# The V product of a sparse-expert layer on TensorE: half of its float32 products split in three float32r products, and the loop around them rebuilt

## The chip, the core and the metric

The kernel runs on one core of one Trainium2 chip. The metric is the device time of one execution in microseconds (us), the median of several runs; lower is better. PE is TensorE, PEld its weight loads, DVE VectorE, ACT ScalarE, POOL GpSimd, and SP the engine that issues most DMAs.

## What is computed

One layer of an encoder runs on 1024 prompt positions and 64 sample positions: a modulated RMS norm, a mixing part (a gated recurrence and a state-space scan), and then a retrieval of experts with product keys. The retrieval is the part that matters here. Each position has 8 heads; each picks 16 of 16384 experts. An expert is one row `u` and one row `v` of 1024 numbers.

```python
gate = jax.nn.softmax(top_s, axis=-1)
act = jax.nn.gelu(jnp.einsum("nd,nhkd->nhk", xb, u_tab[eidx]).astype(jnp.float32))
coef = (gate * act).astype(xb.dtype)
return jnp.einsum("nhk,nhkd->nd", coef, v_tab[eidx])
```

The layer's output is the residual plus a gate times this sum, and a final RMS norm follows. All is float32.

## The kernel before

The time is spent in two parts. Up to about 1226 us the kernel makes everything ahead of the retrieval: mixing, keys, the choice of experts, a table of `u` rows turned round into DRAM, and for the positions that are handled densely a coefficient for each expert and position, stored in `coef_dram`. From 1226 us on one loop of 64 steps makes the retrieval, in two ways side by side.

**Dense way, 576 positions, on PE.** A step `t` takes two blocks of 128 experts, `e` = 0 and 1. Positions stand in two groups of columns, 320 and 256 wide (`DCHUNKS`). `scores(t, j)`, with j = 0 to 3 for the two blocks times the two groups, multiplies the block's `u` rows by the positions' vectors. It makes a float32 product out of three products of type float32r, one instruction each: high part by high part, low by high, high by low (8 x 3 products, line 975). ACT applies gelu from PSUM into the buffer `w` (line 1319), and DVE multiplies `w` by the coefficients (`weigh`). Then `values(g, wp, m)` multiplies the `v` rows of four blocks (two steps, a pair `g`) by `w`: for each of 8 pieces `d` of 128 output channels and each of the two column groups four products of type float32, which run as two instructions each (line 986). The sums lie in four PSUM banks in turn, and DVE adds each of the 16 to `y_sum` in SBUF (`add_up`). In PE's order each `scores(t, j)` is followed by two calls of `values`, one for each column group, of the pair before. I call such a piece, one `scores` and two `values`, a quarter of a step.

**Sparse way, 512 positions, on DVE.** In step `t` eight picks of 128 positions are done. POOL gathers for each the `u` row and the `v` row of every position from DRAM with an indirect DMA of 128 rows of 4 KB (line 599), into a ring of 4 slots for each table. DVE takes the dot product of the `u` row with the position's vector (`dot`, line 1927), ACT applies gelu, and DVE adds the weighted `v` row to `y_rows` (`add_row`, line 1941), one step later. POOL issues the gather for row p + 4 when row p has been used.

**What orders the work.** Every engine runs its program in the order in which it is written, and waits on semaphores. DVE's step interleaves, for each quarter, `weigh`, two `dot`, two `add_up`, two `add_row`; at the end of quarters 0 and 2 it makes the low part of the next `u` rows (`u_rest`, writes `u_lo`), for which ACT makes the high part (`u_first`). SP loads the raw `u` rows, the `v` rows and the coefficients of each step as buffers come free.

**The loop's start and end.** SP loads `u` of step 1 and `v` of steps 0 and 1 after the last coefficients have been stored. At the end PE makes the last 16 `values`; ACT scales `y_sum` by the layer's gate; PE turns the sums back into rows of positions; DVE adds them to the residual, ACT squares, and DVE scales the nine tiles of 128 positions for output.

Of the kernel before, what the change touches and what calls it, by code (L numbers as in the profile page):

```python
# [18 lines left out]
F32 = mybir.dt.float32  # L19
# [6 lines left out]
P = 128  # L26
DM = 1024
# [28 lines left out]
NLINK = 20  # L56
NCAND = 4 * 16 + 12 * 4
# [39 lines left out]
PQ, CB, ITR = 9216, 31232, 47616  # L97
YB, WR, CBD, VR = 31232, 35840, 40448, 42752
# [3 lines left out]
def trunk(nc, A, O):  # L102
    with ExitStack() as ctx:
# [8 lines left out]
        arena = sb("arena", [P, ARENA + NPACK])  # L112
# [20 lines left out]
        u_hi, u_lo = rounded("u_hi", UH, 2048), rounded("u_lo", UR, 2048)  # L133
        yl_hi, yl_lo = rounded("yl_hi", YLH, 4352), rounded("yl_lo", YL, 4352)
# [18 lines left out]
        rms4 = sb("rms4", [P, 30])  # L153
# [161 lines left out]
        def _(sp):  # L315
# [74 lines left out]
            load(ar(X1, 8192).rearrange("p (k d) -> p k d", k=8), A["xp"], "x_again_in")  # L390
            load(ar(X1 + 8192, 1024, DSEQ), A["xs"], "x_again_in")
# [63 lines left out]
            for e in range(2):  # L455
                load(seg(u_in_buf, 1024 * e, 1024), A["ut"][e], f"u_in{e}")
# [1690 lines left out]
```

## Time and profile before

| | |
|---|---|
| runs of the kernel, median | 3094.97 us (3094.22 to 3095.96) |
| profiled execution, its own time | 3102.25 us |
| its span | 3100.5 us |
| PE busy | 2908.3 us, 94% |
| DVE busy | 2553.9 us, 82% |
| POOL busy | 1507.5 us, 49% |
| loop's part of the span | from 1226 us on, about 1874 us |

A profile lists each instruction with its start and length, on each engine. Idle time before an instruction is put down to what released it. PE and DVE pipeline, so that lengths of neighbours can overlap; where the pace of a series is wanted, starts are compared, or pieces of the chain. The DMA row of the page is the busy share of the core's 16 DMA engines.

### The profile page before, as it was taken

How to read it: one execution, taken by the hardware profiler on the slowest of the kernel's cores; microseconds unless marked ns; L12 is line 12 of the kernel's file. 1: busy time of each engine (PE TensorE's matmuls, PEld its weight loads, DVE VectorE, ACT ScalarE, POOL GpSimd, SP SyncE). 2: the span in 40 equal slices, each digit the busy share in tenths (PEclk: the TensorE clock that was granted, in tenths of full speed). 3: DMA queues.
4: the chain of work that ended last, by engine and by line, in shares of the span. 5: the costliest groups of instructions: out<-in, count | busy, mean ns of one | idle time of the engine just before them, and what ended most of it. 6: DMA issues, size and time to landing. Idle time of an engine off the chain costs nothing.

```text
span 3100.5 us, 46585 instructions
## 1 busy us (share of the span) xinstructions
PE 2908.3 (94%) x15724; PEld 2361.7 (76%) x15724; DVE 2553.9 (82%) x5723; ACT 811.0 (26%) x1592; POOL 1507.5 (49%) x1211
## 2 busy tenths in 40 slices
PE   7999799999997677699999999999999999999997
PEld 3566268677775567588888888888888888888886
DVE  6481355478999998699999999999999999999998
ACT  3213230344445798111111111111111111111112
POOL 0000000046675001566677667767676766677662
PEclk8999889999998799799999999999999999999998
DMA  5102730699998367999999999999999999999996
GB/s 209 27 33 43 253 124 31 222 339 323 340 329 335 93 193 241 372 395 389 392 394 392 390 389 398 391 392 387 400 387 394 387 397 390 390 391 394 389 393 250
DMA packets 326544, 959.32 MB, mean 309 GB/s; under 512 B 37264, under 2 KB 119232, under 8 KB 313104
## 3 DMA queue, kind: packets, MB, share of 16 engines
q0 software_dynamic: 147456, 536.94, 44.2%
q1 hardware_dynamic: 158208, 412.59, 36.9%
q10 hardware_dynamic: 20784, 8.67, 1.1%
q8 instruction: 42, 0.69, 0.1%
q14 instruction: 54, 0.44, 0.0%
HBM read 841.10 MB, written 116.85 MB: 309 GB/s over the span
## 4 chain that ended last, share of the span: by engine, by line
PE 82%; DVE 8%; ACT 5%; issue 2%; DMA 1%; ACTq 1%; POOL 0%; DVEq 0%; SPq 0%
PE ps L986 32%; PE ps L975 26%; PE ps L869 6%; PE ps L728 4%; PE ps L852 2%; ACT arena L1280 2%; PE ps L678 2%; ACT arena L1297 2%; PE ps L826 2%; PE ps L835 2%; DVE arena L1385 2%; PE ps L769 2%; DVE arena L1779 1%; PE ps L805 1%; DVE arena L1774 1%
## 5 line engine op out<-in xcount | busy, mean ns | idle before, releaser
L986 PE MATMUL ps<-w,v_rows 128*128 128x320 f32 (+1 forms) x4096 | 1033.6, 405 | 0.0
L986 PEld LDWEIGHTS ps<-w,v_rows 128*128 128x128 f32 x4096 | 763.1, 190 | 203.2
L599 POOL DMA_INDIRECT ring<-in_vt,arena x512 | 701.8, 1371 | 287.4 <-DVE y_rows L1941 193.3
L599 POOL DMA_INDIRECT ring<-u_table,arena x512 | 562.0, 1098 | 456.3 <-DVE ring L1927 218.3
L975 PE MATMUL ps<-h_hi,u_hi 128*128 128x320 f32 (+1 forms) x2048 | 654.1, 319 | 32.3 <-DVE u_lo L1385 30.5
L1941 DVE SCALAR_TENSOR_TENSOR y_rows<-ring,s5c,y_rows 128x1024 f32<-128x1024 f32 x512 | 652.2, 1274 | 2.2 <-DMA ring<-in_vt,arena 2.0
L1927 DVE SCALAR_TENSOR_TENSOR ring<-ring,h_rows 128x1024 f32<-128x1024 f32 x512 | 623.1, 1217 | 18.7 <-DMA ring<-u_table,arena 12.0
L975 PE MATMUL ps<-h_hi,u_lo 128*128 128x320 f32 (+1 forms) x2048 | 607.8, 297 | 0.0
L975 PE MATMUL ps<-h_lo,u_hi 128*128 128x320 f32 (+1 forms) x2048 | 607.7, 297 | 0.0
L1319 ACT ACTIVATE w<-ps 128x320 f32<-128x320 f32 (+1 forms) x256 | 104.6, 410 | 1234.7 <-PE ps L975 1232.5
L975 PEld LDWEIGHTS ps<-h_hi,u_hi 128*128 128x128 f32 x2048 | 390.3, 191 | 39.3 <-DVE u_lo L1385 30.9
L975 PEld LDWEIGHTS ps<-h_lo,u_hi 128*128 128x128 f32 x2048 | 390.3, 191 | 6.4
L975 PEld LDWEIGHTS ps<-h_hi,u_lo 128*128 128x128 f32 x2048 | 389.7, 190 | 0.0
L564 POOL TENSOR_TENSOR arena<-arena 128x2048 f32<-128x2048 f32 (+1 forms) x28 | 73.2, 2637 | 510.3 <-DVE arena L1385 509.8
L1385 DVE TENSOR_TENSOR arena<-arena 128x512 f32<-128x512 f32 (+17 forms) x229 | 186.7, 845 | 157.0 <-ACT arena L1117 62.9
L869 PE MATMUL ps<-h,wq 128*128 128x384 f32 (+1 forms) x768 | 266.8, 471 | 0.9 <-ACT h L307 0.9
L1385 DVE TENSOR_TENSOR y_sum<-ps,y_sum 128x320 f32<-128x320 f32 x496 | 224.0, 452 | 12.5 <-PE ps L986 6.4
L1385 DVE TENSOR_TENSOR w<-w,c_raw 128x320 f32<-128x320 f32 (+1 forms) x256 | 117.5, 460 | 140.7 <-ACT w L1319 140.7
L949 PE MATMUL ps<-arena 128*128 128x128 f32 x1152 | 147.2, 284 | 55.9 <-DVE arena L1910 35.2
L852 PEld LDWEIGHTS ps<-ident,u_turn 128*128 128x128 f32 x1024 | 130.6, 147 | 81.4 <-issue 24.1
L1200 ACT COPY u_turn<-ps 128x512 f32<-128x512 f32 x256 | 147.1, 586 | 166.4 <-PE ps L852 166.1
L949 PEld LDWEIGHTS ps<-arena 128*128 128x128 f32 x1152 | 136.8, 196 | 66.4 <-issue 43.5
(261 smaller groups left out, 3080.4 us busy)
## 6 DMA issues: line engine op xcount, KB each, us to landing
u_turn<-in_ut SPq DMA_DIRECT2D x128, 512.0 KB, 5.6
u_table<-u_turn SPq DMA_DIRECT2D x128, 512.0 KB, 4.3
u_raw<-in_ut SPq DMA_DIRECT2D x128, 512.0 KB, 6.8
v_rows<-in_vt SPq DMA_DIRECT2D x64, 1024.0 KB, 9.3
c_raw<-coef_dram SPq DMA_DIRECT2D x64, 576.0 KB, 8.8
coef_dram<-arena SPq DMA_DIRECT2D x8, 4096.0 KB, 15.9
arena<-in_w_ada SPq DMA_DIRECT2D x24, 1024.0 KB, 7.5
arena<-in_xp SPq DMA_DIRECT2D x2, 4096.0 KB, 12.6
```

The lines of the kernel that those rows point to most:

```text
L599: nc.gpsimd.indirect_dma_start(out=slot(n), out_offset=None, in_=table, in_offset=bass.IndirectOffsetOnAxis(ap=uvi[:, at:at + 1], axis=0)) ...
L728: last = mm(b[:, 0:width], w[:, k, P * m:P * m + P], h[:, k, P * k0:P * k0 + width], start=k == 0, stop=k == 7)
L852: last = nc.tensor.transpose(ps[6 + half][:, P * k:P * k + P], seg(turn_buf[r % NTURN], 512 * half + P * k, P), ident[:, :])
L869: last = mm(ps[q][:, 0:width], w[:, k, :], h2[:, k, P * k0:P * k0 + width], start=k == 0, stop=k == 7)
L949: last = mm(bank[:, j % 4, :], ar(PQ + 2048 * (g % 4) + P * j, P), ar(PQ + 2048 * (g % 4) + 1024 + P * j, P), start=True, stop=True)
L975: last = mm(ps[b0 + j][:, 0:width], w[a][:, k, :], ph[b][:, k, 64 * c0:64 * c0 + width], start=k == 0 and n == 0, stop=k == 7 and n == 2)
L986: last = mm(ps[4 + m % 4][:, 0:width], seg(v_in_buf, 2048 * r + 1024 * e + P * d, P), seg(w_in_buf, ow, width), start=n == 0, stop=n == 3)
L1200: nc.scalar.copy(seg(turn_buf[r % NTURN], 512 * half, 512), ps[6 + half][:, :]).then_inc(s("ut_moved"), 1)
L1319: av(seg(w_in_buf, o, width), ps[b0 + j][:, 0:width], ACT.Gelu_apprx_tanh).then_inc(s("s_gelu"), 1)
L1385: return V.tensor_tensor(o, a, b, op)
L1927: V.scalar_tensor_tensor(out=row, in0=row, scalar=1.0, in1=h_rows[:, bass.ds(1024 * tile_of[0], 1024)], op0=ALU.mult, op1=ALU.mult, accum_ ...
L1941: V.scalar_tensor_tensor(out=y, in0=slot(2 * (p % 4) + 1), scalar=acts[:, u, p:p + 1], in1=y, op0=ALU.mult, op1=ALU.add).then_inc(s("v_row ...
```

## The change

In `values` the `e` = 0 half of the experts is now done as `scores` does it: `v` and `w` are split into high and low parts of type float32r (`v_hi`, `v_lo`, `w_hi`, `w_lo`) and three such products take the place of one float32 product. The `e` = 1 half stays float32. The split costs four new operations a step: on ACT a copy of the 1024 columns of `v` (`v_first`) and two of `w` (`w_first`, 320 and 256 columns); on DVE two subtractions (`w_rest`, 320 and 256); on POOL one subtraction of 1024 columns (`v_rest`).

The sums of the 256-column group now stay in PSUM from the first step to the last, two pieces `d` in each of banks 4 to 7, so that `add_up` is left with the 320-column group alone: 8 for each pair of steps where there were 16. `scores` has two banks where it had four, and `values` of the 320 group has two.

Around the loop: `u` of step 1 and `v` of steps 0 and 1 are loaded before the coefficients are stored; the store of the last coefficients for steps 2 to 63 moves from ACT's queue (two DMAs) to SP's (one); `v` of odd steps is loaded before the second `u` block; DVE's clearing of `y_rows` goes; at the end the 320-column sums come first and are turned back between the 256-column ones; the first three sparse tiles are added to the residual by POOL instead of DVE; and the order of the output tiles changes.

The diff, cut to its core:

```diff
@@ pool
+            def v_rest(t):
+                r = t % 4
+                pool.wait_ge(s("v_hi_ready"), t + 1)
+                nc.gpsimd.tensor_tensor(v_lo[r][:, :], v_row_buf(r)[:, 0:1024], v_hi[r][:, :].bitcast(F32),
+                                        ALU.subtract).then_inc(s("v_lo_ready"), 1)
...
                     if g > 0:
                         v_row(g - 1, p)
+                    if g % 2 and p == 6:
+                        v_rest(g - 1)
+                    if g and g % 2 == 0 and p == 0:
+                        v_rest(g - 1)
+
+            pool.wait_ge(s("g2_out"), 32)
+            pool.wait_ge(s("x1_back"), 16)
+            for t in range(NS - 1):
+                pool.wait_ge(s("v_rows_done"), P * (t + 1))
+                x = seg(x1_buf, 1024 * t, 1024)
+                nc.gpsimd.tensor_tensor(y_tile(t), y_tile(t), g2_buf[:, :], ALU.mult).then_inc(s("x2_first"), 1)
...
+                nc.gpsimd.tensor_tensor(x, y_tile(t), x, ALU.add).then_inc(s("x2_first"), 1)
@@ tensor
                 if not first:
-                    pe.wait_ge(s("s_gelu"), 4 * t + j - 3)
+                    pe.wait_ge(s("s_gelu"), 4 * t + j - 1)
...
-                for n in range(4):
-                    r, e = 2 * wp + n // 2, n % 2
-                    ow = 2304 * wp + 1152 * (n // 2) + ND * e + 64 * c0
-                    last = mm(ps[4 + m % 4][:, 0:width], seg(v_in_buf, 2048 * r + 1024 * e + P * d, P),
-                              seg(w_in_buf, ow, width), start=n == 0, stop=n == 3)
+                if q == 0:
+                    out, begin = ps[2 + d % 2][:, 0:width], True
+                    if not (first and d < 2):
+                        pe.wait_ge(s("y_added"), 8 * g + d - 1)
+                else:
+                    out, begin = ps[4 + d // 2][:, width * (d % 2):width * (d % 2) + width], first and d % 2 == 0
+                for r in (2 * wp, 2 * wp + 1):
+                    for i, (v, w) in enumerate(((v_hi, w_hi), (v_lo, w_hi), (v_hi, w_lo))):
+                        mm(out, v[r][:, P * d:P * d + P], w[r][:, 64 * c0:64 * c0 + width],
+                           start=begin and r % 2 == 0 and i == 0, stop=False, skip_group_check=True)
+                for r in (2 * wp, 2 * wp + 1):
+                    last = mm(out, v_row_buf(r)[:, 1024 + P * d:1024 + P * d + P],
+                              seg(w_in_buf, 1152 * r + ND + 64 * c0, width), start=False, stop=r % 2 == 1,
+                              skip_group_check=True)
@@ tensor, before the values of an even step
                         pe.wait_ge(s("w_weighed"), 16 * k + 8 * (r // 2))
+                        pe.wait_ge(s("v_lo_ready"), 4 * k + 2 * (r // 2))
+                        pe.wait_ge(s("w_lo_ready"), 8 * k + 4 * (r // 2))
@@ tensor, end
+            for d in range(8):
+                values(31, 1, 2 * d)
+            for d in range(8):
+                values(31, 1, 2 * d + 1)
+                if d == 3:
+                    pe.wait_ge(s("s_gelu"), 4 * 64)
+                    pe.wait_ge(s("y_scaled"), 8)
+                    turn_back(4)
+                if d == 5:
+                    pe.wait_ge(s("y_added"), 8 * 32)
+                    turn_back(5)
@@ sync, start
+            for e in range(2):
+                load(ar(U1P + 1024 * e, 1024), A["ut"][2 + e], f"u_in{e}")
+            for t in range(2):
+                load(v_row_buf(t), A["vt"][t], f"v_in{t}")
@@ vector
-            V.memset(y_rows[:, :], 0.0).then_inc(s("y_clear"), 1)
...
+            def w_rest(k, r, q):
+                c0, nb, width = DCHUNKS[q]
+                dve.wait_ge(s("w_hi_ready"), 8 * k + 2 * r + q + 1)
+                tt(w_lo[r][:, 64 * c0:64 * c0 + width], seg(w_in_buf, 1152 * r + 64 * c0, width),
+                   w_hi[r][:, 64 * c0:64 * c0 + width].bitcast(F32), ALU.subtract).then_inc(s("w_lo_ready"), 1)
...
+                    if j > 1:
+                        w_rest(k, r, j - 2)
                     for n in range(2):
                         p = 2 * j + n
                         dot(t, u, p)
-                        add_up(g, 8 * u + p, early)
-                        add_row(t - 1, 1 - u, p)
+                        if n == 0:
+                            add_up(g, 4 * u + j, early)
+                        add_row(t - 1, 1 - u, p, new_tile)
```

What PE does for one quarter after its `scores`, before the change (the last quarter in the loop's body; `w,v_rows` is the product of weights and `v` rows):

```order
L975 MATMUL ps<-h_hi,u_lo 128x256
L982 REGISTER_ALU
L986 MATMUL ps<-w,v_rows 128x320 x4
L982 REGISTER_ALU
L986 MATMUL ps<-w,v_rows 128x256 x4
```

And the 320-column half of the same quarter in the change, with the first rows of the 256-column half (numbers behind names are those of buffers):

```order
L1041 MATMUL ps<-w_hi_84,v_hi_76 128x320
L1041 MATMUL ps<-w_hi_84,v_lo_80 128x320
L1041 MATMUL ps<-w_lo_88,v_hi_76 128x320
L1041 MATMUL ps<-w_hi_85,v_hi_77 128x320
L1041 MATMUL ps<-w_hi_85,v_lo_81 128x320
L1041 MATMUL ps<-w_lo_89,v_hi_77 128x320
L1044 MATMUL ps<-w,v_rows_65 128x320 x2
L1041 MATMUL ps<-w_hi_84,v_hi_76 128x256
```

Two of each four float32 products became six float32r products.

DVE in quarter 2 of a step, before the change, from `weigh` on:

```order
L1385 TENSOR_TENSOR w<-w,c_raw 128x320
L1927 SCALAR_TENSOR_TENSOR ring,s5c<-ring,h_rows 128x1024
L1385 TENSOR_TENSOR y_sum<-ps,y_sum 128x320
L1941 SCALAR_TENSOR_TENSOR y_rows<-ring,s5c,y_rows 128x1024
L1927 SCALAR_TENSOR_TENSOR ring,s5c<-ring,h_rows 128x1024
L1385 TENSOR_TENSOR y_sum<-ps,y_sum 128x256
L1941 SCALAR_TENSOR_TENSOR y_rows<-ring,s5c,y_rows 128x1024
L1385 TENSOR_TENSOR u_lo<-u_raw,u_hi 128x1024
```

And in the change (in this step the sparse sums lie in `h_rows`, the buffer of a tile that is done):

```order
L1500 TENSOR_TENSOR w<-w,c_raw 128x320
L1500 TENSOR_TENSOR w_lo_90<-w,w_hi_86 128x320
L2040 SCALAR_TENSOR_TENSOR ring,s5c<-ring,h_rows 128x1024
L1500 TENSOR_TENSOR y_sum<-ps,y_sum 128x320
L2057 SCALAR_TENSOR_TENSOR h_rows<-ring,s5c,h_rows 128x1024
L2040 SCALAR_TENSOR_TENSOR ring,s5c<-ring,h_rows 128x1024
L2057 SCALAR_TENSOR_TENSOR h_rows<-ring,s5c,h_rows 128x1024
L1500 TENSOR_TENSOR u_lo<-u_raw,u_hi 128x1024
```

A `w_lo` of 320 columns came in ahead of the dots, and the 256-column addition went.

POOL in the loop, before the change, only alternates:

```order
L599 DMA ring<-u_table,arena 128x1024
L599 DMA ring<-in_vt,arena 128x1024
L599 DMA ring<-u_table,arena 128x1024
L599 DMA ring<-in_vt,arena 128x1024
L599 DMA ring<-u_table,arena 128x1024
```

In the change, at the gathers for the picks 6 and 7 of an odd step and 0 of the next:

```order
L632 DMA ring<-u_table,arena 128x1024
L632 DMA ring<-in_vt,arena 128x1024
L651 TENSOR_TENSOR v_lo_80<-v_rows_65,v_hi_76 128x1024
L632 DMA ring<-u_table,arena 128x1024
L632 DMA ring<-in_vt,arena 128x1024
L632 DMA ring<-u_table,arena 128x1024
L632 DMA ring<-in_vt,arena 128x1024
L651 TENSOR_TENSOR v_lo_81<-v_rows_65,v_hi_77 128x1024
L632 DMA ring<-u_table,arena 128x1024
```

Both subtractions of a pair of steps stand within four gathers, and none in the other twelve turns of `u` and `v` gathers.

## Rows read from the trace of the kernel before

**Rows 1.** the page of the kernel before: span, busy time, DMA share and rate by slice

```profile
span 3100.5 us, 46585 instructions
...
PE 2908.3 (94%) x15724; PEld 2361.7 (76%) x15724; DVE 2553.9 (82%) x5723; ACT 811.0 (26%) x1592; POOL 1507.5 (49%) x1211
...
DMA  5102730699998367999999999999999999999996
GB/s 209 27 33 43 253 124 31 222 339 323 340 329 335 93 193 241 372 395 389 392 394 392 390 389 398 391 392 387 400 387 394 387 397 390 390 391 394 389 393 250
...
```

**Rows 2.** stretches: busy time of each engine (x instructions), granted clock, DMA share, GB/s

```profile
...
1270.00:1280.00 10.00, 0.00 (x0) 0.00 (x0) 7.25 (x11) 0.00 (x0) 6.77 (x7) 0.57 1.03 417
1280.00:1290.00 10.00, 2.94 (x11) 2.94 (x12) 7.78 (x11) 0.21 (x1) 5.62 (x4) 0.50 1.02 410
2000.00:2560.00 560.00, 560.00 (x3169) 492.78 (x3168) 511.91 (x773) 74.36 (x139) 391.48 (x318) 1.00 1.00 392
...
```

**Rows 3.** the chain that ended last, from 3015 us: start, length, what

```profile
...
3021.98 2.87 PE ps L975 x24
3024.84 3.88 PE ps L986 x16
3028.72 3.51 PE ps L975 x24
...
3038.98 31.06 PE ps L986 x128
...
```

**Rows 4.** timeline of DVE, one step: start, length, operation, idle before

```profile
...
2005.11 0.42 DVE L1385 TENSOR_TENSOR y_sum<-ps,y_sum 128x256 f32<-128x256 f32 x1
2005.45 1.27 DVE L1941 SCALAR_TENSOR_TENSOR y_rows<-ring,s5c,y_rows 128x1024 f32<-128x1024 f32 x1
...
2007.78 0.42 DVE L1385 TENSOR_TENSOR w<-w,c_raw 128x256 f32<-128x256 f32 x1
2008.11 1.22 DVE L1927 SCALAR_TENSOR_TENSOR ring<-ring,h_rows 128x1024 f32<-128x1024 f32 x1
...
2014.66 0.49 DVE L1385 TENSOR_TENSOR w<-w,c_raw 128x320 f32<-128x320 f32 x1 [1.06 <-ACT w L1319]
2015.07 1.22 DVE L1927 SCALAR_TENSOR_TENSOR ring<-ring,h_rows 128x1024 f32<-128x1024 f32 x1
...
2028.80 0.51 DVE L1385 TENSOR_TENSOR w<-w,c_raw 128x320 f32<-128x320 f32 x1 [1.13 <-ACT w L1319]
...
```

**Rows 5.** waits of POOL from 2000 to 2560 us: total, times, longest

```profile
...
POOL ring L599 <- DVE ring L1927: 61.4, 77, 1.4
POOL ring L599 <- DVE y_rows L1941: 54.0, 76, 0.9
POOL ring L599 <- issue: 53.5, 165, 2.2
```

**Rows 6.** groups of all engines from 650 to 1010 us, each shape by itself

```profile
...
L564 POOL TENSOR_TENSOR arena<-arena 128x2048 f32<-128x2048 f32 x14 | 63.4, 4530 | 510.3 <-DVE arena L1385 509.8
...
L1385 DVE TENSOR_TENSOR arena<-arena 128x128 f32 x6 | 17.4, 2892 | 0.9 <-DVE arena L1861 0.9
...
L1385 DVE TENSOR_TENSOR arena<-arena 128x128 f32<-128x128 f32 x9 | 3.2, 351 | 0.3
...
```

**Rows 7.** groups of all engines from 1056 to 1062 us

```profile
...
L1910 DVE TENSOR_SCALAR arena<-iota,arena 128x128 f32<-128x128 f32 x6 | 5.9, 1044 | 0.0
L585 POOL TENSOR_TENSOR u_lo<-u_raw,u_hi 128x1024 fp32r<-128x1024 f32 x2 | 4.7, 2386 | 67.7 <-ACT u_hi L1273 67.7
...
```

**Rows 8.** DMA issues from 2000 to 2560 us: size and median us to landing

```profile
...
v_rows<-in_vt SPq DMA_DIRECT2D x20, 1024.0 KB, 8.8
...
ring<-u_table,arena POOLq DMA_INDIRECT x159, 8.2
...
```

**Rows 9.** timeline of PE at the start of the loop

```profile
...
1252.42 0.64 PE L975 MATMUL ps<-h_hi,u_hi 128*128 128x320 f32 x1 [11.40 <-DVE u_lo L1385]
...
1287.06 0.63 PE L975 MATMUL ps<-h_hi,u_hi 128*128 128x320 f32 x1 [19.07 <-DVE u_lo L1385]
...
```

More of the change, by code:

```diff
@@ L56 @@
 NLINK = 20
+BACK = {4: 0, 5: 2, 6: 4, 7: 6, 8: 0}
+LAST = (0, 1, 2, 4, 5, 3, 6, 7, 8)
 NCAND = 4 * 16 + 12 * 4
@@ L133, in trunk @@
         u_hi, u_lo = rounded("u_hi", UH, 2048), rounded("u_lo", UR, 2048)
+        v_hi = [rounded(f"v_hi{r}", VH012 + 1024 * r if r < 3 else VH3, 1024) for r in range(4)]
+        v_lo = [rounded(f"v_lo{r}", (V01 if r < 2 else V23) + 2048 * (r % 2), 1024) for r in range(4)]
+        w_hi = [rounded(f"w_hi{r}", WH + ND * ((r + 2) % 4), ND) for r in range(4)]
+        w_lo = [rounded(f"w_lo{r}", WR + 1152 * r, ND) for r in range(4)]
         yl_hi, yl_lo = rounded("yl_hi", YLH, 4352), rounded("yl_lo", YL, 4352)
@@ L1304, in _ @@
             for e in range(2):
-                u_first(0, e)
+                u_first(0, e, first=True)
             move_block(1, 1, fresh=True)
@@ L1988, in _ @@
                 if p == 4:
-                    u_rest(1, 0)
+                    u_rest(1, 0, U1P)
             for j in range(4):
                 weigh(0, 0, j)
-            u_rest(1, 1)
+            u_rest(1, 1, U1P + 1024)
+            dve.wait_ge(s("u_lo_ready0"), 2)
+            for q in range(2):
+                w_rest(0, 0, q)
             weights_of(0, 0)
@@ L2000, in _ @@
                     u_rest(2, 0)
+            for q in range(2):
+                w_rest(0, 1, q)
             dve.wait_ge(s("coef_rest"), 16)
@@ L2060, in _ @@
                 last.then_inc(s("x2_done"), 1)
+            for d in range(8):
+                add_up(31, d, last=True)
+                add_row(63, 1, d)
+            dve.wait_ge(s("ssq4"), 3)
+            ts(rms4[:, 10:13], rms4[:, 0:3], 1.0 / DM, EPS, ALU.mult, ALU.add).then_inc(s("mean_squares_ready"), 1)
+            dve.wait_ge(s("v_in0"), 16 * 16 + 32)
+            dense_sum(4)
+            dve.wait_ge(s("roots_ready"), 8)
+            link(V.reciprocal(rms4[:, 20:23], rms4[:, 20:23]))
+            dve.wait_ge(s("params_in"), 48)
+            for i in range(3):
+                scaled_out(i)
+            dense_sum(5)
+            dve.wait_ge(s("g2_out"), 32)
+            sparse_sum(NS - 1)
+            for t in (6, 7, 8):
+                dense_sum(t)
             dve.wait_ge(s("ssq4"), NTILE)
@@ L2067, in _ @@
             link(V.reciprocal(rms4[0:DSEQ, 28:29], rms4[0:DSEQ, 28:29]))
-            for t in range(NS - 1, NTILE):
-                scaled_out(t)
+            for i in range(3, NTILE):
+                scaled_out(i)
 _ROWS = {"pack": (P, NPACK), "b_ada": (2, 6 * DM), "ddiag": (GS, DL), "w_ada": (DM, 6 * DM), "xp": (P, L, DM),
```

240 lines of the change are left out of this document (138 added, 102 removed).

## The prediction

> **What bounds the kernel now.** I read the page first. PE is busy 94% of the span, DVE 82%, POOL 49%, and from the seventeenth slice on the DMA row stands at nine tenths or more with 370 to 400 GB/s, except in the last slice [rows 1]. So three things may be near their limit in the loop, and the busy shares don't say which one paces it. Then I took one stretch of the steady loop, 2000 to 2560 us: PE is busy all of 560 us at the full granted clock, DVE 511.91, POOL 391.48, and the DMA engines' share is 1.00 at 392 GB/s [rows 2]. The chain gives PE's pace: `scores` of 320 and 256 columns take 3.51 and 2.87 us, the two `values` of a quarter 3.88 [rows 3]. A step is thus 2 x (3.51 + 3.88) + 2 x (2.87 + 3.88) = 28.28 us, and the 560 us hold 19.8 of them. DVE waits for gelu at the start of each half step, 1.06 and 1.13 us [rows 4], so it is the faster one: 511.91 / 19.8 = 25.85 us of work in 28.28 [rows 2]. PE paces the loop, with two others close behind.
>
> **PE's part of the change.** A float32r product costs 3.51 / 24 = 0.146 us with 320 columns and 2.87 / 24 = 0.120 with 256 [rows 3]. In a quarter half of the 3.88 us goes, 1.94, and 6 x 0.146 + 6 x 0.120 = 1.60 comes. That saves 0.34 us a quarter and 1.37 a step: PE could do a step in 26.91. The change between the two types costs nothing that I can see: the 3.88 between two `scores` already holds both changes. `scores` with two banks still waits for a gelu two quarters back, long done. The loop has 62 steps with `values` in it, so PE alone would give 85 us. What follows asks who stops it.
>
> **DVE.** Four additions of 256 columns go, 0.34 us each by their starts (2005.11 to 2005.45), 1.36 a step. Two `w_rest` come; I price them like `weigh` of the same width, by starts: 0.41 (2014.66 to 2015.07) and 0.33 (2007.78 to 2008.11) [rows 4]. 25.85 - 1.36 + 0.74 = 25.23 us.
>
> Then there is what POOL does to DVE. A subtraction of 1024 columns takes POOL 2.39 us; in those few microseconds six small DVE operations that take about 0.33 each averaged 1.04, and PE behind them waited [rows 7]. Earlier, while POOL ran 4.53 us operations, DVE's tensor_tensor operations of 128x128 averaged 2.89 us in one form, where another form of that size took 0.35 [rows 6]. So a DVE operation can stand still for as long as POOL's runs. No row shows a `dot` or `add_row` beside such a POOL operation; between 0 and the full 2.39 us a step I take the full length, since both read two operands in SBUF, as those tensor_tensor operations do. DVE's step: 25.23 + 2.39 = 27.62.
>
> The Trainium skill, "SBUF — State Buffer", section "Who interferes with whom", says that a DVE instruction with two SBUF inputs contends with a GpSimd instruction that reads SBUF, that the lock lasts a whole instruction, and that whoever issues first wins. By it `dot` and `add_row` are blocked and the additions out of PSUM are not, and the sum would be the same 27.62; it speaks against the change, since without the lock it would be 25.23.
>
> **POOL.** A step has 391.48 / 19.8 = 19.77 us of gathers [rows 2], 53.5 / 19.8 = 2.70 of issue gaps and 115.4 / 19.8 = 5.83 of waits for DVE [rows 5]. An issue gap is 53.5 / 165 = 0.32 us; I count as much of each of the 7.7 waits a step as fixed handover, and 3.35 us is then spare. `v_rest` takes 2.39 + 0.32 = 2.71, and up to a DVE operation of 1.2 us more, 0.6 on average, if it must wait for one. POOL's own step is 28.28 - 3.35 + 2.71 = 27.64 at best and 28.24 with that wait.
>
> **DMA.** 392 GB/s x 28.28 us is 11.09 MB a step. In the stretch 1270 to 1290 us, where DVE waited for rows and every slot was asked for, the engines moved 417 and 410 GB/s [rows 2]. So a step can be fed in 26.6 to 27.0 us; at 392 it could not go below 28.28. The Trainium skill, "DMA: Bandwidth & Descriptors", section "iDMA fabric — 4 AXI ports for 8 engines, asymmetric across TPBs", lists 408.7 GB/s for a load stream alone; by it the floor would be 27.1 us.
>
> **The step.** PE 26.91, DMA 27.0, DVE 27.62, POOL 27.64 to 28.24. I take 27.85, between DVE's value and POOL's upper one. That is 0.43 us less, and 62 x 0.43 = 27 us. What is late next: both `v_rest` of a pair stand within four gathers, in quarters 1 and 2 of the odd step. DVE is held 4.8 us there, its `u_lo` for the next step comes late, and PE, at the head of `scores`, waits for it a microsecond or two once in two steps. ACT's copies have room: ACT is busy 74.36 of 560 us [rows 2]; its new waits are for `weigh` of a quarter before and for `v` rows landed a step ago. The waits for `v_lo` and `w_lo` ahead of an even step's `values` come after DVE's last quarter and 7 us after its gelu, so a lag of up to 5 us is covered.
>
> **Start of the loop.** PE waits 11.40 us before `scores` of step 1 and 19.07 before those of step 2 [rows 9], in a time when the DMA engines are full [rows 2]. 3.15 MB (`u` of step 1, `v` of steps 0 and 1) leave it for a time when the DMA row had half its share free; at 413 GB/s that is 7.6 us. I take 8, with bounds 0 (another load or DVE is what is late) and 19, the second wait whole. The clearing of `y_rows` was covered by the wait for the first rows: nothing.
>
> **End.** The last `values` shrink from 31.06 [rows 3] to 8 x 3.54 = 28.3 us, and three tiles leave DVE's list. Against that PE's second half now waits for DVE's additions with two banks, `add_row` is in their way, and POOL's six operations of 2.39 us, 14.3 in all, stand beside them and hold ACT's squares. I take 0, with bounds -9 and +5.
>
> **Sum.** -27 - 8 + 0 = -35 us. The trace's own execution took 3102.25 us for a span of 3100.5; the median of the runs is 7.3 lower, 3094.97. The forecast for the median is 3060 us.
>
> **The rivals.** *Forecast, 0.45*: a step of 27.6 to 28.24, that is 3045 to 3087 us. A measurement of this kernel tells 0.2% or 6 us from no change.
>
> *POOL doesn't hold DVE, 0.22.* For: the gathers are POOL operations too and run beside DVE all the time, and rows 6 compare two forms. Against: rows 7. Then the DMA engines or PE pace, about 27.1 us: 62 x 1.18 + 8 = 81, so 3014 us.
>
> *The DMA engines are full at 392 GB/s, 0.15.* For: a share of 1.00 throughout, and a gather that needs 8.2 us from issue to landing [rows 8]. Against: 410 to 417 where more was asked. Then the step stays 28.28, PE waits where it worked, and only the start is left: 3087 us.
>
> *Slower, the ring runs dry, 0.15.* A slot is used again after four picks, 14.14 us. Of these a `dot` of 1.22 [rows 4], a handover of 0.6 and the landing's 8.2 [rows 8] leave 4.1 us. The two `v_rest` with their waits put 2 x 3.3 = 6.6 us between four gathers. If DVE has to wait for the 2.5 us over, besides being held, its pair costs 2 x 27.62 + 2.5, a step 28.87: +37 - 8 = +29, so 3124 us. For it: POOL's spare time is nearly gone. Against: while POOL's operation runs DVE stands still too, so the ring isn't emptied meanwhile. It decides from 0.8 us a step of such waits on, where the 0.66 of DVE's gain and the start's 0.13 a step are used up.
>
> *Start or end off by more than their bounds, 0.03.*
>
> **The numbers.** Faster holds the forecast but for its edge (0.43), the lock's absence (0.22), over half of the full DMA case, whose 8 us lie just beyond the bound (0.08), and a bit of the rest: 0.74. The same: 0.10. Slower: the dry ring and half the rest, 0.16. Leaving some 0.08 below and 0.12 above, the range is 3015 to 3096 us.
>
> **What would show it.** Right: in the steady loop a step of 27.6 to 28.2 us; PE with 0.5 to 1 us of idle time a step, most of it once in two steps and put down to `u_lo`; `dot` or `add_row` in odd steps with lengths of 2 to 3.6 us beside POOL's `v_rest`; hardly a wait of DVE for gelu; POOL busy over 80%; 395 to 402 GB/s. Wrong: `dot` and `add_row` keep 1.2 us throughout and GB/s rises over 405; or the rate stays 392 and waits name gathers; or DVE waits for `ring` by over 0.8 us a step. The first `scores` of step 2 should start near 1279 us.

## The result, and the profile after

The changed kernel is slower by a third of a per cent: 3107.07 us (median; 3099.91 to 3111.26) against 3095.96 us of the kernel before in the same comparison, a ratio of 1.0034 (95% interval 1.0027 to 1.0042). That is small, but clear of the noise. The forecast was 3060 us, with a range up to 3096. The two profiled executions differ by less, 3107.07 to 3102.25 us, or 4.8 us of span, and only these 4.8 can be placed in the traces. All views here are of the changed kernel unless said otherwise.

From the page, beside [rows 1]:

```profile
span 3105.3 us, 48275 instructions
...
PE 2850.8 (92%) x16748; PEld 2393.5 (77%) x16748; DVE 2634.4 (85%) x5588; ACT 912.1 (29%) x1792; POOL 1707.1 (55%) x1281
...
GB/s 208 30 31 43 254 126 40 214 338 327 336 327 330 144 182 247 358 389 383 393 383 393 401 384 393 398 385 400 396 390 395 383 392 391 388 399 381 395 403 211
```

PE is busy 57.5 us less and the kernel takes longer. The steady loop as in [rows 2] and one stretch of 3 us in it (busy us of PE, PEld, DVE, ACT, POOL, then PE's granted clock, DMA share, GB/s):

```profile
2000.00:2560.00 560.00, 541.22 (x3492) 503.04 (x3491) 538.50 (x734) 103.26 (x196) 447.74 (x337) 0.99 1.00 392
...
2080.00:2083.00 3.00, 3.00 (x14) 3.00 (x13) 3.00 (x7) 0.00 (x0) 2.41 (x2) 0.50 1.00 411
```

The waits from 2000 to 2560 us (us in total, times, longest), of all engines but ACT, beside [rows 5]:

```profile
POOL ring L632 <- issue: 83.5, 275, 0.9
PEld ps L1027 <- issue: 24.3, 15, 2.8
PE ps L1027 <- DVE u_lo L1500: 18.8, 12, 2.4
POOL ring L632 <- DVE ring L2040: 15.2, 15, 1.3
POOL ring L632 <- DVE h_rows L2057: 11.4, 17, 0.8
DVE w L1500 <- ACT w L1408: 6.7, 12, 1.0
DVE ring L2040 <- DMA ring<-u_table,arena: 6.6, 7, 1.5
DVE h_rows L2057 <- DMA ring<-in_vt,arena: 5.8, 10, 1.0
```

PE, never idle in this stretch before, now waits for `u_lo`. POOL's waits for DVE fell from 115.4 us to 26.6: it has hardly any time to spare. Why `u_lo` is late shows on DVE's and POOL's timelines of an odd step, from the `weigh` of its quarter 2 to the `u_lo` at the quarter's end (start, length, operation):

```profile
2010.91 2.28 DVE L1500 TENSOR_TENSOR w<-w,c_raw 128x320 f32<-128x320 f32 x1 [0.31 <-ACT w L1408]
...
2017.40 1.30 DVE L2057 SCALAR_TENSOR_TENSOR h_rows<-ring,s5c,h_rows 128x1024 f32<-128x1024 f32 x1
2018.62 3.38 DVE L1500 TENSOR_TENSOR u_lo<-u_raw,u_hi 128x1024 fp32r<-128x1024 f32 x1
```

```profile
2010.29 2.55 POOL L651 TENSOR_TENSOR v_lo<-v_rows,v_hi 128x1024 fp32r<-128x1024 f32 x1
...
2018.40 2.52 POOL L651 TENSOR_TENSOR v_lo<-v_rows,v_hi 128x1024 fp32r<-128x1024 f32 x1
2021.07 1.76 POOL L632 DMA_INDIRECT ring<-u_table,arena  x1
```

The `weigh` takes 2.28 us where 0.49 was normal [rows 4], and `u_lo` 3.38 where 1.21 is. Both end only after POOL's subtraction has ended, 0.35 and 1.08 us later. PE then waits for this `u_lo`:

```profile
2022.13 0.41 PE L1027 MATMUL ps<-h_hi,u_hi 128*128 128x320 f32 x1 [1.79 <-DVE u_lo L1500]
```

Between steps 4 and 60 POOL makes 56 of these subtractions, and beside each of them exactly one DVE operation is longer, the one that comes next: 28 times `weigh`, 26 times `u_lo`, once `w_lo` and once a `dot`. The `add_row` that is under way when POOL starts keeps 1.30 us. Of PE's 34 waits for `u_lo` 26 come behind a held one, 48.7 of 54.3 us.

PE's timeline one pair of steps later shows what such a wait costs beyond itself:

```profile
2078.62 0.41 PE L1027 MATMUL ps<-h_hi,u_hi 128*128 128x320 f32 x1 [2.40 <-DVE u_lo L1500]
...
2079.75 0.31 PE L1027 MATMUL ps<-h_lo,u_hi 128*128 128x320 f32 x1
...
2080.32 0.47 PE L1027 MATMUL ps<-h_lo,u_hi 128*128 128x320 f32 x1
2080.59 0.47 PE L1027 MATMUL ps<-h_hi,u_lo 128*128 128x320 f32 x1
```

The products start 0.147 us apart at first and then 0.27: the granted clock is 0.50 from 2080 to 2083, the lower of TensorE's two levels.

The pace, by the gelu that opens steps 2, 4 and 60 and the last gelu of all on ACT's timeline, in the kernel before and then in the changed one:

```profile
1293.06 0.44 ACT L1319 ACTIVATE w<-ps 128x320 f32<-128x320 f32 x1 [4.67 <-PE ps L975]
...
1349.62 0.44 ACT L1319 ACTIVATE w<-ps 128x320 f32<-128x320 f32 x1 [2.04 <-PE ps L975]
...
2933.35 0.44 ACT L1319 ACTIVATE w<-ps 128x320 f32<-128x320 f32 x1 [2.00 <-PE ps L975]
...
3039.02 0.38 ACT L1319 ACTIVATE w<-ps 128x256 f32<-128x256 f32 x1 [6.31 <-PE ps L975]
```

```profile
1285.15 0.42 ACT L1408 ACTIVATE w<-ps 128x320 f32<-128x320 f32 x1
...
1345.77 0.44 ACT L1408 ACTIVATE w<-ps 128x320 f32<-128x320 f32 x1
...
2932.86 0.44 ACT L1408 ACTIVATE w<-ps 128x320 f32<-128x320 f32 x1
...
3034.35 0.39 ACT L1408 ACTIVATE w<-ps 128x256 f32<-128x256 f32 x1 [5.67 <-PE ps L1027]
```

Between steps 4 and 60 a step takes 1587.09 / 56 = 28.34 us, before 28.28. The steps aren't equal: from an even gelu to the odd one it is 26.84 us, from odd to even 29.84, on average between steps 4 and 60.

The end, from the chain that ended last (the short pieces between these are left out):

```profile
3035.58 2.60 POOL v_lo L651
3038.32 14.91 DMA ring<-in_vt,arena
...
3054.86 1.28 DVE h_rows L2057
3056.45 1.29 DVE h_rows L2057
3058.00 0.94 POOL ring L632
3058.96 2.39 POOL y_rows L673
3061.41 3.25 POOL x L675
3064.66 3.33 POOL h_rows L673
3068.06 3.24 POOL x L675
3071.30 3.32 POOL h_rows L673
3074.67 2.41 POOLq L106
3077.10 1.15 ACT square L1460 x2
```

A gather of a `v` row needs 14.91 us behind the `x1` loads, and POOL's six operations follow one another. From the last gelu to the end of the trace it takes 70.9 us, before 61.4.

**Where the 4.8 us are.** Step 2's gelu comes 7.9 us earlier (1293.06 before), but 4.1 of these are gone by step 4. Steps 4 to 60 take 3.4 us more. The steps after 60 up to the last gelu take 4.2 less, which includes the phase of the uneven steps. The end takes 9.5 more. -3.9 + 3.4 - 4.2 + 9.5 = 4.8. The other 6 us between the medians' difference and this are not placed. The profiled execution of the kernel before was 6.3 us over its median, that of the changed one was the median itself, and ahead of the loop executions differ by up to 10.5 us (the first `dot` starts at 1219.2 to 1229.7 us in the profiled executions of this study).

### The profile page after: what moved, and what is told of

It is laid out like the page before. It is cut to its first block, busy times and chain, and to the rows that moved or that the text cites. A ratio compares the mean times of both kernels' runs of the same rounds, so it can differ in the third digit from the quotient of the medians.

```text
span 3105.3 us, 48275 instructions
## 1 busy us (share of the span) xinstructions
PE 2850.8 (92%) x16748; PEld 2393.5 (77%) x16748; DVE 2634.4 (85%) x5588; ACT 912.1 (29%) x1792; POOL 1707.1 (55%) x1281
## 4 chain that ended last, share of the span: by engine, by line
PE 39%; POOL 23%; DVE 13%; DMA 10%; issue 9%; ACT 5%; ACTq 0%; DVEq 0%; POOLq 0%; SPq 0%
POOL ring L632 19%; PE ps L1027 8%; DMA ring<-in_vt,arena 8%; PE ps L921 6%; PE ps L1044 4%; PE ps L780 4%; POOL v_lo L651 3%; PE ps L1041 3%; PE ps L904 2%; ACT arena L1359 2%; PE ps L730 2%; ACT arena L1376 2%; PE ps L878 2%; PE ps L887 2%; DVE h_rows L2057 2%
## 5 line engine op out<-in xcount | busy, mean ns | idle before, releaser
L632 POOL DMA_INDIRECT ring<-u_table,arena x512 | 669.2, 1307 | 339.9 <-PE ps L1001 155.9
L1044 PE MATMUL ps<-w,v_rows 128*128 128x320 f32 (+1 forms) x2048 | 582.5, 407 | 0.0
L2057 DVE SCALAR_TENSOR_TENSOR h_rows<-ring,s5c,h_rows 128x1024 f32<-128x1024 f32 x381 | 498.4, 1308 | 22.5 <-DMA ring<-in_vt,arena 22.4
L1044 PEld LDWEIGHTS ps<-w,v_rows 128*128 128x128 f32 x2048 | 359.9, 190 | 55.1 <-issue 1.0
L1041 PE MATMUL ps<-w_hi,v_hi 128*128 128x320 f32 (+1 forms) x1024 | 367.4, 359 | 14.8 <-DVE w_lo L1500 8.9
L1041 PE MATMUL ps<-w_hi,v_lo 128*128 128x320 f32 (+1 forms) x1024 | 302.8, 296 | 0.0
L1041 PE MATMUL ps<-w_lo,v_hi 128*128 128x320 f32 (+1 forms) x1024 | 302.7, 296 | 0.0
L1041 PEld LDWEIGHTS ps<-w_hi,v_hi 128*128 128x128 f32 x1024 | 194.2, 190 | 38.1 <-issue 9.9
L1500 DVE TENSOR_TENSOR u_lo<-u_raw,u_hi 128x1024 fp32r<-128x1024 f32 x124 | 211.1, 1703 | 8.5 <-ACT u_hi L1351 8.5
L1041 PEld LDWEIGHTS ps<-w_hi,v_lo 128*128 128x128 f32 x1024 | 194.3, 190 | 20.3 <-issue 0.4
## 6 DMA issues: line engine op xcount, KB each, us to landing
coef_dram<-arena SPq DMA_DIRECT2D x8, 4096.0 KB, 15.9
```

Of the source, the lines that this page charges most:

```text
L632: nc.gpsimd.indirect_dma_start(out=slot(n), out_offset=None, in_=table, in_offset=bass.IndirectOffsetOnAxis(ap=uvi[:, at:at + 1], axis=0)) ...
L1041: mm(out, v[r][:, P * d:P * d + P], w[r][:, 64 * c0:64 * c0 + width], start=begin and r % 2 == 0 and i == 0, stop=False, skip_group_check= ...
L1044: last = mm(out, v_row_buf(r)[:, 1024 + P * d:1024 + P * d + P], seg(w_in_buf, 1152 * r + ND + 64 * c0, width), start=False, stop=r % 2 == ...
L1500: return V.tensor_tensor(o, a, b, op)
L2057: V.scalar_tensor_tensor(out=y, in0=slot(2 * (p % 4) + 1), scalar=acts[:, u, p:p + 1], in1=y, op0=ALU.mult, op1=ALU.add).then_inc(s("v_row ...
```

## The experiments

A step is measured between the gelus of steps 4 and 60. "PE waits" and "ring waits" (DVE waiting for gathered rows) are of 2000 to 2560 us, "end" is from the last gelu. The ratios are of medians of 4 to 15 runs; step, waits, rate and end are of one profiled execution each.

| | us, median | ratio (95%) | step | PE waits | ring waits | GB/s | end |
|---|---|---|---|---|---|---|---|
| before | 3095.96 | | 28.28 | 0 | 0 | 392 | 61.4 |
| changed | 3107.07 | 1.0034 (1.0027 to 1.0042) | 28.34 | 18.8 | 12.4 | 392 | 70.9 |
| e1_rest_on_dve | 3075.66 | 0.9928 (0.9911 to 0.9944) | 27.90 | 15.8 | 1.1 | 398 | 67.8 |
| e2_half_v | 3075.94 | 0.9929 (0.9913 to 0.9946) | 27.84 | 14.7 | 5.5 | 377 | 71.8 |
| e3_both | 3070.83 | 0.9915 (0.9899 to 0.9932) | 27.80 | 15.2 | 0 | 380 | 67.8 |
| e4_before_half_v | 3098.59 | 1.0006 (0.9997 to 1.0016) | 28.28 | 0 | 0 | 374 | 61.5 |
| e5_pool_filled | 3111.65 | 1.0042 (1.0027 to 1.0056) | 28.52 | 21.1 | 9.3 | 389 | 69.0 |
| e9_quarters_tail | 3040.19 | 0.9812 (0.9793 to 0.9831) | 27.23 | 2.6 | 15.9 | 407 | 67.7 |
| e12_e9_pool_filled | 3090.31 | 0.9980 (0.9968 to 0.9992) | 28.04 | 15.2 | 26.2 | 397 | 68.4 |
| e16_rests_apart | 3109.36 | 1.0041 (1.0024 to 1.0058) | 28.33 | 22.2 | 17.9 | 391 | 71.1 |
| e6_tail_on_dve | 3103.42 | 1.0017 (1.0006 to 1.0028) | 28.30 | 18.6 | 12.1 | 391 | 68.3 |
| e13_changed_rows_last | 3112.87 | 1.0055 (1.0040 to 1.0071) | 28.34 | 17.7 | 10.2 | 391 | 77.5 |
| e7_late_loads | 3114.87 | 1.0055 (1.0037 to 1.0073) | 28.31 | 17.5 | 9.9 | 392 | 71.9 |
| e10_rows_last | 3032.97 | 0.9797 (0.9783 to 0.9810) | 27.33 | 5.9 | 18.7 | 405 | 63.1 |
| e15_e10_half_v | 3014.91 | 0.9736 (0.9720 to 0.9753) | 26.91 | 0 | 7.3 | 392 | 62.0 |

**Theories.** L: POOL's `v_rest`, by its time or by holding DVE, ate the loop's gain. D: the DMA engines are full at 392 GB/s.

### e1_rest_on_dve

```diff
+            def v_rest(k, r):                       # DVE's
+                dve.wait_ge(s("v_hi_ready"), 4 * k + r + 1)
+                tt(v_lo[r][:, :], v_row_buf(r)[:, 0:1024], ...
...
+                    if r % 2 and j in (1, 3):
+                        v_rest(k, r - (j == 1))
```

> The changed kernel with v_rest moved from POOL to DVE: 1.21 us of DVE a step, as u_lo of the same size takes, in place of a held DVE (27.3 us busy a step now). PE's own pace is 26.91 us. Theory L (POOL's v_rest, by its own time and by holding DVE, keeps the step at 28.34 us): the step falls to 26.9 to 27.2 us, all of 62 steps, and the time to about 3107 - 62 x 1.25 = 3030 us; GB/s rises to 405 to 412. Theory D (the DMA engines are full at 392 GB/s, 11.09 MB a step): the step stays at 28.2 to 28.4 us and the time at 3105 us, with the waits now for the ring or the loads.

Measured: a step of 27.90 us at 398 GB/s. D as put is refuted, since all bytes moved faster. L got a third of the 1.25 us that it promised, but the edit had a flaw of its own: what PE waits for has changed to the second of the two new subtractions:

```profile
PE ps L1037 <- DVE v_lo L1496: 15.8, 10, 2.1
```

### e2_half_v, e3_both, e4_before_half_v

These three load only the first 1024 of the 2048 columns of `v` in the loop. They leave out 0.52 MB a step, and the `e` = 1 half multiplies old rows.

```diff
-            def load_v(t, r):
-                load(v_row_buf(r), A["vt"][bass.ds(t, 1)].rearrange("t p n -> (t p) n"), f"v_in{r}")
+            def load_v(t, r, n=2048):     # the loop gives n=1024
+                load(v_row_buf(r)[:, 0:n], A["vt"][bass.ds(t, 1)].rearrange("t p n -> (t p) n")[:, 0:n], f"v_in{r}")
```

> The changed kernel with the V loads of the loop cut to the first 1024 of their 2048 columns (the second expert of each pair multiplies old rows): 0.52 MB a step less, 10.57 of 11.09 MB. Theory D: the step follows the bytes, 10.57 / 0.392 = 27.0 us, or DVE's 27.3, and the time falls to about 3107 - 62 x 1.0 = 3045 us. Theory L: the step stays at 28.3 us, 3107 us, and the rate falls to 10.57 / 28.3 = 373 GB/s.

> v_rest on DVE and the V loads halved, in the changed kernel (the second expert of each pair multiplies old rows). Either theory: PE's pace, 26.9 to 27.0 us a step, 3020 to 3025 us. If it is no faster than the better one of the two single edits, that edit alone had removed the bound; if neither edit alone helps and both do, two bounds stand side by side.

> The kernel before with the same cut of its V loads (old rows for the second expert of each pair). PE paces that kernel by its own products, 28.28 us a step, so both theories say 28.28 us a step and 3095 us, with the rate down to 374 GB/s. If it gets faster, the kernel before was held by the DMA engines as well.

Measured: e2's step is 27.84, neither theory's value, and e3's 27.80 is hardly better than either single edit. e4 behaves as a kernel that PE paces: 28.28. So in the changed kernel fewer bytes are worth 0.50 us a step and e1's edit 0.45. e3 doesn't tell whether the two add up: in e1 and e3 alike PE waits for `v_lo` (15.8 and 15.2 us), whose place was my own choice, and that wait hides what fewer bytes would give. In e2 it is still `u_lo`:

```profile
PE ps L1027 <- DVE u_lo L1500: 14.7, 10, 2.3
```

### e5_pool_filled, e12_e9_pool_filled

```diff
+                    if (g % 2 and p == 6) or (g and g % 2 == 0 and p == 0):
+                        pool.wait_ge(s("v_hi_ready"), g)
+                        for n in range(8):
+                            if g > 1 or n:
+                                pool.wait_ge(s("pad"), 8 * (g - 1) + n)
+                            nc.gpsimd.memset(iota[:, :], 0.0).then_inc(s("pad"), 1)
```

> As e1, v_rest on DVE, but POOL does a chain of eight small memsets (0.2 to 0.3 us each) where v_rest stood, so that its time is spent as in the changed kernel and no SBUF operand is read by it. If what matters is that POOL's v_rest holds DVE (the lock), this stays at e1's 27.90 us a step and 3076 us. If it is POOL's own time, late gathers that follow from it and ring waits of DVE, the step goes back to 28.3 us, 3105 us, with DVE waiting for ring by 0.6 us a step. In between: both count.

> As e9, but POOL does the chain of eight memsets (2.07 us, twice in two steps) where v_rest stood in the changed kernel. DVE's operations keep their lengths beside them (they did in e5), so it shows POOL's time without any hold on DVE. If POOL's time is enough to lose the loop's gain, the step goes from 27.23 to 28.0 to 28.4 us and the time to 3090 to 3110 us. If the hold is the larger part, it stays under 27.6 us, 3063 us.

Measured: e5 28.52 us a step where e1 has 27.90 (e5's profiled execution was 11 us over its median), e12 28.04 where e9, described below, has 27.23. The medians agree for e12 and e9: 3090.31 - 3040.19 = 50 us, or 0.81 a step. Eight memsets take 2.07 us. DVE's operations beside them keep their lengths: between steps 4 and 60 of e12 these were 54 `v_lo` of 1.21 us and 27 `weigh` of 0.47 to 0.49. Only one `u_lo` stood there, but none was held, by the groups from 2000 to 2560 us (busy us, mean ns):

```profile
L1494 DVE TENSOR_TENSOR u_lo<-u_raw,u_hi 128x1024 fp32r<-128x1024 f32 x40 | 48.6, 1215 | 0.0
```

In the changed kernel the same group has

```profile
L1500 DVE TENSOR_TENSOR u_lo<-u_raw,u_hi 128x1024 fp32r<-128x1024 f32 x40 | 68.0, 1700 | 0.0
```

So POOL's time alone, with no hold on DVE, costs 0.81 us a step (e9 to e12). The gathers start later, the ring waits of DVE grow from 15.9 to 26.2 us, and PE waits for `u_lo`. What the hold adds isn't measured by itself. The changed kernel is 0.30 us a step longer than e12, but that is a net value: there DVE is held for 2.0 us a step, and doesn't do the subtractions itself, 1.21. No run has the hold without POOL's time.

### e16_rests_apart

```diff
-                    if g % 2 and p == 6:
+                    if g % 2 and p == 4:
                         v_rest(g - 1)
```

> The changed kernel with the first of POOL's two v_rest one gather pair earlier in the odd step, so that four picks and not two lie between them. If it is their nearness that makes the gathers late, DVE's ring waits (12.4 us in 560) and PE's wait for u_lo (18.8) fall and the step goes from 28.34 to 27.9 us or less, 3080 us. If the sum of POOL's time is what counts, the step stays at 28.2 to 28.4 us and the time at 3100 to 3107 us.

Measured: 28.33 us, no change. PE's waits are twice as many (24 for 12) and shorter (1.2 us at most), 22.2 us in sum for 18.8, so it isn't the nearness of the two. Now it is mostly a `u_lo` that is held (beside 49 of the 56 subtractions between steps 4 and 60), and 49 of PE's 60 waits stand behind a held one. The granted clock stays at 1.00 throughout these steps, and the step is no shorter for it.

### e6_tail_on_dve, e13_changed_rows_last

e6, at the end, takes the six operations from POOL:

```diff
                 add_up(31, d, last=True)
+                if d < NS - 1:
+                    x = seg(x1_buf, 1024 * d, 1024)
+                    tt(y_tile(d), y_tile(d), g2_buf[:, :], ALU.mult).then_inc(s("x2_first"), 1)
+                    dve.wait_ge(s("x2_first"), 2 * d + 1)
+                    tt(x, y_tile(d), x, ALU.add).then_inc(s("x2_first"), 1)
                 add_row(63, 1, d)
```

e13 changes only the place of the rows:

```diff
                 add_up(31, d, last=True)
-                add_row(63, 1, d)
+            for p in range(4):
+                add_row(63, 1, p)
...
                 scaled_out(i)
+            for p in range(4, 8):
+                add_row(63, 1, p)
             dense_sum(5)
```

> The changed kernel with the three early sparse sums of the end on DVE, in the gaps in which it waits for the last V rows (3.07 and 4.03 us), in place of POOL's six operations. Theory: those six (3058.96 to 3077.08 us) and the add_row operations that they hold (3.0 to 3.9 us in place of 1.28) are what made the end 9.6 us longer; DVE's additions would end near 3062 and the rest follow: 8 to 12 us less, 3095 to 3099 us. Rival: the last gathers, 14.9 us behind the x1 loads, set the end, and under 3 us are saved. The loop stays at 28.3 us a step.

> The changed kernel with nothing but DVE's order at the end as in e10 (its sparse sums stay on POOL). If the rows in flight were the cause of the 9.6 us that the end lost, 6 to 10 us come back: 3098 us. If POOL's sums are the rest of it, they now stand beside DVE's dense sums and give less than 3 us, 3104 to 3107 us.

Measured: e6 gains 2.7 us of the end, e13 loses 6.6. e6's rival was right; e13 went outside both expectations. Its ACT timeline shows why:

```profile
3069.82 1.06 ACT L1460 ACTIVATE square<-x 128x1024 f32<-128x1024 f32 x1 [9.00 <-POOL x L675]
```

POOL's sums stand in its queue behind the gathers of rows 4 to 7, and these wait for the slots that rows 0 to 3 free. Whoever delays the rows delays POOL's sums. Together, in e10, DVE's sums and the later rows are worth 7.8 us of the end.

### e7_late_loads

```diff
-            table_stored(sp, 0)
-            for e in range(2):
-                load(ar(U1P + 1024 * e, 1024), A["ut"][2 + e], f"u_in{e}")
-            for t in range(2):
-                load(v_row_buf(t), A["vt"][t], f"v_in{t}")
...
             for t in range(2):
                 load_c(t, t)
+            table_stored(sp, 0)
+            for e in range(2):
+                load(ar(U1P + 1024 * e, 1024), A["ut"][2 + e], f"u_in{e}")
+                load(v_row_buf(e), A["vt"][e], f"v_in{e}")
```

> The changed kernel with only its early loads put back: u of step 1 and v of steps 0 and 1 are loaded after the coefficients of the first steps, as in the kernel before. If the early loads are what gained 8.0 us at the start, the gelu of step 2 comes 7 to 9 us later than in the changed kernel and the time is 3115 us; if the gain came from the single store of the last coefficients or from the shorter work ahead, no more than 2 us are lost.

Measured: 7.8 us slower, and step 2's gelu, counted from the first `dot`, 9.1 us later. So the start gained by the early loads. How much of it stays varies: in the four profiled executions with the changed kernel's start (changed, e2, e6, e13) step 2's gelu comes 59.2 to 60.7 us behind the first `dot` and step 4's 119.8 to 122.2, where the kernel before has 66.6 and 123.2, and e7 68.3 and 129.8. In e16, whose first subtraction on POOL comes earlier in step 1, nothing of the gain is seen: 67.0 and 123.1.

### e9_quarters_tail, e10_rows_last

e9 is e1 with `j in (1, 2)`, and e6's end; e10 adds e13's places of the rows, with the early sparse sums between the additions.

> v_rest on DVE after the quarters 1 and 2 of the odd step (e1: 1 and 3), and the tail of e6. PE waited 1.58 us a pair for v_lo in e1. If that wait was only the place of the second subtraction, the step falls from 27.90 to 27.1 to 27.3 us, and with the tail's 10 us the time to 3076 - 45 - 8 = 3023 us. If DVE is simply late at that place (u_lo or w_lo is then what PE waits for), the step stays at 27.7 to 27.9 us and the time at 3065 us.

> As e9, but at the end DVE does all eight additions out of PSUM first, the early sparse sums between them, then rows 0 to 3 of the last gathers, and rows 4 to 7 only before dense_sum(5). From the last gelu to the end takes 67.7 us in e9, 61.4 in the kernel before. If what is late in the end is that PE's last products wait behind additions that stand behind rows still in flight, it falls to 57 to 61 us and the time to 3031 to 3034 us. If the x1 loads or the normalization set it, it stays at 66 us or more, 3039 us. Loop: 27.2 us a step.

Measured: e9 27.23 us a step. One quarter earlier for one subtraction is worth 0.67 us, and against the changed kernel L now has 1.11 of its 1.25 us: taking `v_rest` off POOL gives back nearly the whole loss, once DVE does it at a good place. The rate is 407 GB/s. e9's time missed its forecast, 3040 us for 3023: of the 8 us put on the end 3.2 came. e10's end is 4.6 us shorter than e9's (63.1, where 57 to 61 was expected), and it is 2.0% faster than the kernel before (0.9797), the fastest version here that leaves nothing out.

### e15_e10_half_v

As e2's edit, in e10, with the same columns left out.

> e10 with the V loads of the loop halved as in e2 (old rows for the second expert of each pair). e10 takes 27.33 us a step at 405 GB/s, with 18.7 us of ring waits in 560, 0.42 over PE's own 26.91. If the DMA engines are what is left, the ring waits go and the step falls to 26.9 to 27.0 us, 3010 us. If DVE's own work is (537 of 560 us busy), it stays at 27.2 to 27.4 us and 3030 us.

Measured: 26.91 us a step, and PE is busy all of the stretch:

```profile
2000.00:2560.00 560.00, 560.00 (x3661) 524.61 (x3660) 546.30 (x791) 110.99 (x208) 432.23 (x334) 1.00 1.00 392
```

What e10 still lacks, 0.42 us a step, goes with fewer bytes.

## Why the prediction was wrong

**PE's part: right.** 26.91 us a step was worked out from [rows 3]; e15, where PE never waits, measures 26.91.

**DVE's work: right in size.** Forecast 25.23 plus 2.39 of hold, 27.62. The stretch has 538.50 / 19.76 = 27.25 us a step. The longer lengths of `u_lo` (1700 for 1215 ns, 40 of them) and `weigh` (960 for 490 with 320 columns, 39; 469 for 414 with 256, 40) make 40 us, 2.0 a step, and 25.2 are left. In the loop it was not `dot` or `add_row` that was held, as I had taken, but `weigh` and `u_lo`, which come next in DVE's program when POOL starts. At the end, beside POOL's sums, `add_row` is held too, up to 3.87 us for 1.28:

```profile
3058.55 3.87 DVE L2057 SCALAR_TENSOR_TENSOR h_rows<-ring,s5c,h_rows 128x1024 f32<-128x1024 f32 x1
```

The Trainium skill, "SBUF — State Buffer", section "Who interferes with whom", says that a DVE instruction with two SBUF inputs contends with a GpSimd instruction that reads SBUF and not with one that only writes it. The traces agree with both halves: `u_lo` takes 3.38 us beside `v_rest`, `v_lo` of the same size 1.21 beside memsets.

**POOL's part: mis-sized little.** Forecast 27.64 to 28.24; POOL's work and gaps are (447.74 + 83.5) / 19.76 = 26.9, with 1.35 of waits for DVE, 28.2 in all.

**"I take 27.85, between DVE's value and POOL's upper one": the step that failed.** I took the step as hardly more than the largest of four separate times: over DVE's work it leaves 0.23 us for waiting. In the changed kernel DVE has 27.25 us of work a step, waits 0.63 for gathered rows and 0.34 for gelu, and 0.12 go in gaps too short to have a cause: 28.34 in all. So DVE's work was over-sized by 0.4 and its waiting, 1.09, under-sized by 0.9. The prediction named the mechanism, DVE held 4.8 us in a pair of steps, `u_lo` late, and PE waiting "a microsecond or two once in two steps". That came true, and so did the sign, "0.5 to 1 us of idle time a step": it was 0.95. The rate, though, stayed at 392 GB/s, where 395 to 402 was to show that the forecast was right. But the waits run in a ring. PE, which has no second buffer for `u_lo`, waits for DVE; DVE waits for PE's gelu; and POOL, with a subtraction in its queue, is late with rows for DVE. The wait that the forecast lets one engine absorb comes back on another.

The same 28.34 from PE's side are 26.91 and these waits between steps 4 and 60:

```profile
PE ps L1027 <- DVE u_lo L1500: 54.3, 34, 2.4
```

The next products start 0.26 us later than after no wait, besides the wait itself, 9 us in all. After 11 of the waits the clock fell to its lower level and the next 24 products took 1.54 us longer, 17 us. That is 80 of the (28.34 - 26.91) x 56 = 80 us that PE lost. The clock's 17 us are a part of this account and not a cause of the step: in e16 the clock never fell and the step is 28.33, with 62 us of waits.

**What is shown of the cause, and what isn't.** `v_rest` on POOL is what cost the loop its gain: with it on DVE, at a good place, the step is 27.23 (e9 against the changed kernel, 1.11 us). It costs in two ways. POOL's time alone, with no hold, costs 0.81 (e9 against e12): POOL asks for rows later, and DVE's waits for rows grow. The hold stands directly ahead of 26 of PE's 34 waits in the changed kernel. Both ways show in that trace: one step before each of these 26, DVE had waited for rows, for 0.3 to 2.9 us in sum. In the four cases where this was under 0.4 us PE waited 1.16 us, and in the ten where it was over 1.4 us PE waited 2.15 to 2.40. The shares of the two aren't separated by a run. Nor was a second buffer for `u_lo` tried. The place of one DVE operation (e1 against e9, 0.67) and fewer bytes (e2 against the changed kernel, 0.50) weigh as much: each is more than the gain that I had forecast (0.43).

**The rivals.** "The ring runs dry" had the sign. Its price was too high: ring waits of 0.63 us a step, not 1.25, and a step of 28.34, not 28.87. By its own mark, 0.8 us of such waits, the kernel would have stayed faster. Nor are ring waits enough to make a kernel slow: e9 has more of them (15.9 us in the stretch for 12.4) and is the faster by 1.11 us a step. "The DMA engines are full at 392 GB/s" had the step right (28.28) for a wrong reason: 407 GB/s in e9. The same rate of 392 before and after only follows from the same step. My floor of 27.0 us from short stretches at 413 GB/s held; the Trainium skill's 408.7 GB/s ("DMA: Bandwidth & Descriptors", section "iDMA fabric — 4 AXI ports for 8 engines, asymmetric across TPBs") lies at what e9 kept up over 560 us.

**Start: -8 forecast, 3.9 kept at step 4.** Step 2's gelu is 7.9 us earlier, but that it meets the 8 is partly luck. The first products of step 2 start 12.7 us earlier than before, at 1274.34 us where I had named 1279. ACT makes their gelu only at 1285.15, because in its program the gelu of the sparse dot products stands ahead, and the row for the last of these came late (DVE waited 7.03 us for it). For the same row PE waits for the new `w_lo`, which stands behind that `dot` in DVE's program, a wait that I hadn't priced at the start:

```profile
1287.46 0.61 PE L1041 MATMUL ps<-w_hi,v_hi 128*128 128x320 f32 x1 [7.76 <-DVE w_lo L1500]
```

**End: "I take 0", bounds -9 and +5; measured +9.5, the other term that failed.** I had named `add_row` in the way of the additions and POOL's 14.3 us. I had not seen that they chain: rows behind the `x1` loads, the slots behind the rows, POOL's sums behind the slots' gathers, ACT's squares behind the sums. Terms that I took as alternatives stood in a row. The traces' +4.8 us is 40 over the forecast's -35: 27.5 in the 56 steps measured (+3.4 for 56 x -0.43), 9.5 here, about 5 up to step 4, and 2.5 less after step 60.

## What to carry to other kernels

When the step's busy times of three engines and the transfers all lie within 5% of each other, the largest is a lower bound and not an estimate; price the waits in the order of the ring, and look first at a single buffer (here `u_lo`), where lateness shows. Before work goes to an engine that "has time", see what stands behind it in that engine's queue and what it holds on others: 2.07 us more of POOL's time twice in two steps, with nothing held, cost 0.81 us a step. And one operation's place within a step can be worth more (0.67 us) than the gain that was forecast for the change (0.43).

## What the runs showed of the hardware

- A DVE operation with two SBUF operands that comes up while POOL subtracts from SBUF stands still: a `u_lo` ended 1.08 us after POOL's 2.5 us were over, a `weigh` of 320 columns 0.28 to 0.36 us after. One that was under way when POOL started kept its length (`add_row` 1.30 us). Beside eight POOL memsets `weigh` kept 0.47 to 0.49 and `v_lo` 1.21 us. Additions out of PSUM kept 0.48 us beside the memsets and beside POOL's sums at the end.
- After 11 of 34 waits of PE, all 11 between 1.7 and 2.4 us long, the granted clock fell to 0.50. The products slowed 0.4 to 1.6 us after PE had resumed, for about 3 us. After seven others as long it stayed at 1.00, and so it did after all 60 waits of e16.
- The DMA engines kept up 407 GB/s over 560 us with three quarters of the bytes in gathered rows (331 gathers of 512 KB). Their share was 0.98 at 374 GB/s (e4), 1.00 at 392 and 1.02 at 407 (e9), so a share of 1.00 doesn't tell that no more can be moved.
- A gather that needs 8 us in the loop (median 8.1, at most 11.7 from 2000 to 2560 us) needs 14.9 us behind 4.5 MB of plain loads (1536, 2560 and 256 KB).
